# A bias table built with TensorE instead of VectorE, twelve modulation pieces moved to an earlier stage, and GpSimd's norm started later

## The chip, the cores and the metric

The kernel runs as one program on one core of a Trainium2 chip. The core has five engines, each with its own instruction stream: TensorE (PE, matmuls), VectorE (DVE), ScalarE (ACT), GpSimd (POOL) and SyncE (SP), which here only issues DMA transfers. The metric is the device time of one execution in microseconds, and less is better.

## The reference

A chain of six layers over one sequence of 256 tokens with 1024 features. The first block is four mixers with a residual and an RMS norm each: a conformer convolution, a forgetting attention, a short convolution, and a second conformer convolution. The second block has two layers, each of a token mixer (two attentions, gated and merged) and a convolutional feed-forward net, with a layer norm behind each and with a shift, scale and gate that come from a product with the large matrix `w_ada`:

```python
x = first_block(x, ...)                       # stages a0, b, c, a1
for l in range(DEPTH_2):                      # 2 layers: stages m0, f0, m1, f1
    mod = jax.nn.silu(c) @ w_ada[l] + b_ada[l]
    sh1, sc1, g1, sh2, sc2, g2 = jnp.split(mod[:, None, :], 6, axis=-1)
    h = x * (1.0 + sc1) + sh1
    y = token_mixer(h, positions, rel_bias, ...)
    x = layer_norm_2(DEEPNORM_ALPHA * x + g1 * y, ln1_g[l], ln1_b[l])
    h = x * (1.0 + sc2) + sh2
    y = conv_ffn(h, w_up[l], conv_w[l], conv_b[l], w_down[l])
    x = layer_norm_2(DEEPNORM_ALPHA * x + g2 * y, ln2_g[l], ln2_b[l])
```

What the change is about is the position bias of the first of the two attentions. For each of 8 heads, a query at position q and a key at position k get `rel_bias[t5_bucket(q - k)]`, where the bucket is the distance itself below 16, grows with its logarithm up to 128, and ends at 31:

```python
bias = rel_bias[t5_bucket(q_pos[:, :, None] - k_pos)]
logits = jnp.einsum('bqhd,bqkhd->bqkh', q, k_sel) * a_scale + bias
```

All arithmetic is in float32, and both layers of the second block use the same table.

## The kernel before

Activations stay on the chip; the weights, 332 MB, stream through it once. They are cut into 637 pieces, most of 128 rows by 1024 columns (0.52 MB). SP issues them in the order of a list that the functions `plan_a`, `plan_b`, `plan_c`, `plan_m` and `plan_f` write, into six buffers `raw`, so each transfer waits until the piece six places earlier has been used. A piece is one of three kinds. A **split** piece goes through ACT, which writes its high part `wh` (L107), and DVE, which writes the rest, `wl` = raw - wh (L114); TensorE then makes three matmuls of each 128x128 tile (high by high, high by low, low by high; L98), 24 matmuls of 256 columns for a piece. A **plain** piece is multiplied once, in slower float32. An **ada** piece belongs to `w_ada`: no matmul, but one DVE instruction over 128x1024 (L124 `raw<-raw,cb`) that multiplies by silu(c) and sums. Layer 0 of `w_ada` has 48 such pieces in stages b (28) and c (20); layer 1's 48 come in m0 (8, one behind each of its `qk` pieces) and f0 (40: two behind each `u` pair from i = 2 on). Which pieces lie where in the list is the whole schedule: ACT and DVE run through it up to three pieces ahead of the piece that TensorE is at (`feed_act`, `feed_dve`), and the wait for a semaphore before each use does the rest. Each engine's order is written out by hand, one function for each engine and stage (`pe_b`, `act_b`, `dve_b` and so on); an instruction behind a waiting one on its engine waits too.

The stages in order are a0, b, c, a1, m0, f0, m1, f1. Each begins with an **entry**: the norm, TensorE's transposes of X into PSUM (L101), then for each of 8 tiles a high part on ACT and a low part on DVE (`XS<-tmp,XS`, L114), and only then full matmuls. In m and f stages DVE's part of the entry is `dve_enter`. Stage b has values v0 to v2 (`values`), then keys and queries (`k`, `q`: eight pairs of pieces each), then v3, then 19 attention steps. Stage c runs over i = 0, 2, ..., 14; stages f over i = 0, 2, ..., 20, two halves each.

**The bias table.** `bias_step` (L1074) makes it in 305 DVE instructions: distances and buckets in 17, then for each of 32 buckets one mask of 128x384 and for each of 8 heads `table += mask * rel_bias` (128x384). They are fitted between other DVE work by calls `self.bias(dve, n)`: 6 behind each of v0 to v3, 5 behind each k and q pair, 2 + 2 in each attention step, 5 at each of four points of every i of stage c. In the trace they are the L124 groups `B<-B,C` and `B<-sc,C,B`, with some L119. The first reader is m0's attention (`dve_m`).

**GpSimd's norm.** Behind stages m0, f0 and m1, `pool_norm` (L1699) makes the next residual out of the normalised row: eight instructions X*g and X+b over 128x512. It waits for the next stage's transposes, which read X. The lines of the trace are `POOL L114 X<-X,B`.

**The head.** SP issues x in two halves, then one block of constants (2619 columns, 1.3 MB), the positions, six weight pieces and c. The first DVE work, the small `sm` instructions of the first norm, waits for the constants.

Of the kernel before, what the change touches and what calls it, by code (L numbers as in the profile page):

```python
# [347 lines left out]


class Net:  # L350

# [718 lines left out]
    def bias_views(self):  # L1070
        b = self.m["B"][2]
        return b[:, 0:3072].rearrange("p (h s) -> p h s", h=8), b[:, 3072:3456], b[:, 3456:3840]

    def bias_step(self, dve, n):  # L1074


        s, m = self.s, self.m
        Bz, dist, bk = self.bias_views()
        eq = [m["sc"][:], dist]
        up = s["bias"]  # L1080
        if n == 0:
            pf = self.tmp[5][:, 0:T + 2]
            dve.tensor_copy(pf, m["pos"][:]).then_inc(up.up("pf"), 1)
            dve.wait_ge(*up["pf"])
            for o, k, w in ((0, 0, 128), (128, 1, 256)):
                dve.ts(dist[:, o:o + w], pf[:, 0:w], pf[:, T + k:T + k + 1], -1.0, ALU.subtract,
                       ALU.mult).then_inc(up.up(("n", k)), 1)
            dve.wait_ge(*up["n", 1])
            dve.ts(dist, dist, 0.0, None, ALU.max, None).then_inc(up.up("n"), 1)
            dve.wait_ge(*up["n"])  # L1090
            dve.ts(bk, dist, 15.0, None, ALU.min, None).then_inc(up.up(("bk", 0)), 1)
        elif n <= 16:
            dve.wait_ge(*up["bk", n - 1])
            dve.stt(bk, dist, float(bucket_starts()[n - 1]), bk, ALU.is_ge, ALU.add).then_inc(up.up(("bk", n)), 1)
        else:
            b, h = (n - 17) // 9, (n - 17) % 9 - 1
            if h < 0:
                dve.wait_ge(*up["bk", 16])
                if b >= 2:
                    dve.wait_ge(*up["add", b - 2, 7])  # L1100
                dve.ts(eq[b % 2], bk, float(b), None, ALU.is_equal, None).then_inc(up.up(("mask", b)), 1)
            else:
# [1357 lines left out]
```

## Time and profile before

| | us |
|---|---|
| median of 3 runs | 2084.36 (2083.13 to 2084.97) |
| the profiled execution | 2082.0 |
| its span in the trace | 2080.2 |
| PE busy | 1895.7 (91%) |
| weight load (PEld) busy | 1702.1 (82%) |
| DVE busy | 1620.2 (78%) |
| ACT busy | 1079.7 (52%) |
| POOL busy | 301.1 (14%) |
| mean granted TensorE clock | 0.962 |
| bytes moved | 342 MB, 165 GB/s, the queue that carries them busy 50% |

The stages, by the moments at which one ends and the next begins: a0 0 to 254, b to 610, c to 858, a1 to 1102, m0 to 1360, f0 to 1603, m1 to 1862, f1 to 2080. TensorE is the busiest engine throughout. The numbers of one engine's busy time are sums over the whole span, and an engine that is idle behind another's result in one stage may be the bound in the next; so the profile is best read stage by stage, with the chain of waits to say who waited for whom. "Clock" is the TensorE clock that was granted, as a share of full speed (1.00 is 2.4 GHz, 0.50 is 1.2 GHz).

### The profile page before, as it was taken

Reading aid. Unit: us, or ns where it says so; the run is one execution under the profiler, and the core shown is the slowest. Engines: PE = TensorE matmul, PEld = TensorE weight load, DVE = VectorE, ACT = ScalarE, POOL = GpSimd, SP = SyncE. Lnnn points to the kernel's source line nnn. Section 1 sums busy time; section 2 is a strip of 40 time slices with the busy share of each in tenths; the row PEclk is TensorE's granted clock in tenths of the full one; section 3 lists DMA queues with packets and bytes.
Section 4 is the critical chain, followed back from the end, with each engine's and each line's share of the span. In section 5 each row is a group of like instructions: output and inputs, shape, how many; then the busy total and the mean of one; then the engine's idle time right before and its main releaser. Section 6 shows DMA issues by size and latency. Waiting matters only on the chain.

```text
span 2080.2 us, 32564 instructions
## 1 busy us (share of the span) xinstructions
PE 1895.7 (91%) x12370; PEld 1702.1 (82%) x12370; DVE 1620.2 (78%) x3041; ACT 1079.7 (52%) x1928; POOL 301.1 (14%) x380
## 2 busy tenths in 40 slices
PE   7897999989999999989979988988887987889997
PEld 6897888868889899889968876877886986779996
DVE  6988788978889998599976866778888576686666
ACT  6887644423354444478855444444445444454554
POOL 3876000000000000087800000020001000010000
PEclk9998999989999999999989999999999999999998
DMA  6344455634446776344535632537775352344652
GB/s 219 124 162 132 162 183 186 229 111 142 132 139 219 236 236 204 112 139 145 171 111 162 206 110 82 183 121 268 273 266 181 122 151 78 103 161 153 206 189 71
DMA packets 93756, 342.29 MB, mean 165 GB/s; under 512 B 10400, under 2 KB 10528, under 8 KB 92960
## 3 DMA queue, kind: packets, MB, share of 16 engines
q1 hardware_dynamic: 93600, 340.20, 49.9%
q8 instruction: 99, 1.62, 0.3%
q14 instruction: 57, 0.47, 0.1%
HBM read 339.11 MB, written 1.05 MB: 164 GB/s over the span
## 4 chain that ended last, share of the span: by engine, by line
PE 56%; DVE 30%; ACT 11%; issue 2%; DMA 0%; POOL 0%; SPq 0%; DVEq 0%; ACTq 0%
PE ps L98 55%; DVE wl L114 9%; ACT tmp L104 6%; DVE ps L124 5%; DVE tmp L124 3%; ACT wh L107 3%; DVE B L124 2%; DVE XS L114 2%; DVE tmp L114 1%; DVE B L114 1%; DVE tmp L119 1%; DVE raw L124 1%; ACT B L104 1%; DVE sm L136 1%; PE ps L101 1%
## 5 line engine op out<-in xcount | busy, mean ns | idle before, releaser
L98 PE MATMUL ps<-XS,wh 128*128 128x256 f32 (+1 forms) x5072 | 955.2, 290 | 39.9 <-DVE wl L114 27.4
L98 PEld LDWEIGHTS ps<-XS,wh 128*128 128x128 f32 (+1 forms) x5072 | 807.9, 195 | 65.4 <-issue 40.6
L114 DVE TENSOR_TENSOR wl<-raw,wh 128x1024 fp32r<-128x1024 f32 (+1 forms) x493 | 591.8, 1228 | 180.5 <-ACT wh L107 180.5
L98 PE MATMUL ps<-XS,wl 128*128 128x256 f32 (+1 forms) x2536 | 726.6, 287 | 0.0
L107 ACT CAST wh<-raw 128x1024 fp32r<-128x1024 f32 (+1 forms) x493 | 496.0, 1038 | 98.6 <-PE ps L98 92.8
L98 PEld LDWEIGHTS ps<-XS,wl 128*128 128x128 f32 (+1 forms) x2536 | 495.4, 195 | 0.0
L114 POOL TENSOR_TENSOR B<-B,tmp 128x236 f32<-128x236 f32 (+10 forms) x352 | 268.3, 800 | 775.1 <-ACT tmp L104 775.1
L98 PE MATMUL ps<-wh,os 128*128 128x512 f32 x864 | 291.0, 405 | 27.8 <-DVE os L114 18.9
L124 DVE SCALAR_TENSOR_TENSOR ps<-B,C,ps 128x254 f32<-128x254 f32 (+17 forms) x576 | 224.5, 469 | 8.3 <-ACT ps L104 8.3
L98 PEld LDWEIGHTS ps<-wh,os 128*128 128x128 f32 x864 | 167.9, 194 | 67.0 <-DVE os L114 20.8
L98 PE MATMUL ps<-wl,os 128*128 128x512 f32 x432 | 173.4, 401 | 0.0
L98 PE MATMUL ps<-B,raw 128*128 128x256 f32 x768 | 168.2, 379 | 0.0
L98 PEld LDWEIGHTS ps<-B,raw 128*128 128x128 f32 x768 | 145.1, 190 | 19.2
L114 POOL TENSOR_TENSOR X<-X,B 128x512 f32<-128x512 f32 x24 | 32.6, 1371 | 798.0 <-PE ps L101 797.0
L104 ACT ACTIVATE tmp<-B,C 128x236 f32<-128x236 f32 (+10 forms) x352 | 142.7, 477 | 8.7 <-POOL B L114 8.2
L124 DVE SCALAR_TENSOR_TENSOR tmp<-ps,C,tmp 128x254 f32<-128x254 f32 (+1 forms) x176 | 72.7, 475 | 89.4 <-ACT tmp L104 89.4
L104 ACT ACTIVATE B<-ps 128x512 f32<-128x512 f32 (+2 forms) x86 | 49.8, 584 | 154.9 <-PE ps L98 154.3
L104 ACT ACTIVATE tmp<-ps,C 128x256 f32<-128x256 f32 x88 | 45.0, 561 | 148.5 <-PE ps L98 148.5
L124 DVE SCALAR_TENSOR_TENSOR raw<-raw,cb 128x1024 f32<-128x1024 f32 x96 | 116.2, 1218 | 0.0
L104 ACT ACTIVATE tmp<-ps 128x384 f32<-128x384 f32 (+2 forms) x129 | 64.9, 510 | 95.6 <-PE ps L98 80.4
L98 PE MATMUL ps<-wh,XS 128*128 128x512 f32 x320 | 100.3, 391 | 0.5 <-DVE wl L114 0.4
L98 PEld LDWEIGHTS ps<-wl,os 128*128 128x128 f32 x432 | 84.4, 195 | 15.5
(155 smaller groups left out, 1950.2 us busy)
## 6 DMA issues: line engine op xcount, KB each, us to landing
raw<-in_w SPq DMA_DIRECT2D x623, 512.0 KB, 4.4
raw<-in_w SPq DMA_DIRECT2D x12, 384.0 KB, 3.9
B<-in_ln SPq DMA_DIRECT2D x4, 1024.0 KB, 6.8
C<-in_cst SPq DMA_DIRECT2D x1, 1309.5 KB, 8.2
X<-in_x SPq DMA_DIRECT2D x2, 512.0 KB, 4.6
out_x<-X SPq DMA_DIRECT2D x4, 256.0 KB, 2.5
cb<-in_cb SPq DMA_DIRECT2D x1, 512.0 KB, 13.2
raw<-in_w SPq DMA_DIRECT2D x2, 256.0 KB, 3.3
```

Source lines behind the costliest of these rows:

```text
L98: return NOTHING if self.e is None else self.e.matmul(*a, **k)
L101: return NOTHING if self.e is None else self.e.transpose(*a)
L104: return NOTHING if self.e is None else self.e.activation(*a, **k)
L107: return NOTHING if self.e is None else self.e.copy(*a)
L114: return NOTHING if self.e is None else self.e.tensor_tensor(o, a, b, op)
L119: return self.e.tensor_scalar(o, a, s1, s2, op0) if op1 is None else self.e.tensor_scalar(o, a, s1, s2, op0, op1)
L124: return self.e.scalar_tensor_tensor(out=o, in0=a, scalar=s, in1=b, op0=op0, op1=op1, **k)
L136: return NOTHING if self.e is None else self.e.tensor_reduce(o, a, AX, ALU.max)
```

## The change

Four parts.

1. **The table by TensorE.** Positions now come as 128x320: columns 0 to 255 hold the position of each query, the other 64 hold keys, four in a column group, each repeated over 32 partitions. A mask is one DVE instruction, 128 partitions (4 keys x 32 buckets) by 128 queries: is (query - key) at least the start of the partition's bucket? The constants `rblk` hold for each bucket the step of `rel_bias` from the bucket below, so one float32 matmul of a mask (stationary, 128x128) with `rblk` (moving, 32 columns) gives the bias of 4 keys by 8 heads for 128 queries. 96 masks and 96 matmuls make the table, through a ring of 6 mask buffers; every 16 matmuls fill one PSUM bank, and ACT copies it out (`act_bias`, six times). 32 masks stand on DVE ahead of stage a0's first norm (their matmuls are the first of TensorE's program, 16 in each of PSUM banks 6 and 7), and 64 stand in stage b, four behind each k and q pair (bank 3). All 305 former instructions are gone; the attention of m0 now waits for the sixth copy.
2. **The head's transfers.** The positions and 209 columns of constants (`NFIRST`) go first, then x, two weight pieces, the other 2219 columns, four weight pieces, c.
3. **Twelve ada pieces of layer 1** move from the end of f0 (i = 16, 18, 20 have none now) into stage c, where 32 of 32 places are filled instead of 20.
4. **GpSimd's norm** waits for `xlow[nxt, 7]`, the last of the next entry's low parts, instead of the transposes.

The places at which the instructions move are these. DVE at its very start, before the change: the small instructions of the first norm come first, then its application to X and the entry.

```order
L119 TENSOR_SCALAR sm<-sm 128x2
L124 SCALAR_TENSOR_TENSOR sm<-sm 128x2
L130 RECIPROCAL sm<-sm 128x2
L114 TENSOR_TENSOR sm<-sm 128x2
L124 SCALAR_TENSOR_TENSOR sm<-sm 128x2 x2
L119 TENSOR_SCALAR tmp<-X,sm 128x512 x2
L119 TENSOR_SCALAR B<-ps,C 128x256 x8
L114 TENSOR_TENSOR XS<-B,XS 128x256 x8
```

After the change, the same place (`B<-B,C` and `sc<-B,C` of 128x128 are masks; the rows left out repeat the pair):

```order
L131 CAST B<-pos 128x320
L118 TENSOR_TENSOR C<-C 128x32
L123 TENSOR_SCALAR B<-B,C 128x128 x3
L123 TENSOR_SCALAR sc<-B,C 128x128 x3
...
L123 TENSOR_SCALAR B<-B,C 128x128 x2
L123 TENSOR_SCALAR sm<-sm 128x2
L128 SCALAR_TENSOR_TENSOR sm<-sm 128x2
L134 RECIPROCAL sm<-sm 128x2
L118 TENSOR_TENSOR sm<-sm 128x2
L128 SCALAR_TENSOR_TENSOR sm<-sm 128x2 x2
```

32 masks and two conversions now stand ahead of the first norm. Next, TensorE in the k and q part of stage b, after the change; `ps<-tmp,C 16x256` are the row sums for the norm of k, which closed a pair before, too:

```order
L102 MATMUL ps<-XS,wh 128x256 x2
L102 MATMUL ps<-XS,wl 128x256
L102 MATMUL ps<-tmp,C 16x256 x2
L102 MATMUL ps<-C,B 128x32 x3
L102 MATMUL ps<-C,sc 128x32
L102 MATMUL ps<-XS,wh 128x256 x2
L102 MATMUL ps<-XS,wl 128x256
```

Four matmuls of 32 columns with a mask as stationary now follow them. DVE at the end of v3 in stage b, before (`B<-ps` is v3's own evacuation, `B<-B,C,ps 128x256` the scaling of k and q for a head, on which the first attention step waits):

```order
L124 SCALAR_TENSOR_TENSOR raw,mod<-raw,cb 128x1024
L127 COPY B<-ps 128x512
L119 TENSOR_SCALAR B<-B 128x384
L124 SCALAR_TENSOR_TENSOR B<-B,C 128x384 x5
L124 SCALAR_TENSOR_TENSOR B<-B,C,ps 128x256 x2
L124 SCALAR_TENSOR_TENSOR B<-B,C 128x384 x2
L124 SCALAR_TENSOR_TENSOR B<-B,C,ps 128x256 x2
```

and after:

```order
L128 SCALAR_TENSOR_TENSOR raw,mod<-raw,cb 128x1024
L131 COPY B<-ps 128x512
L128 SCALAR_TENSOR_TENSOR B<-B,C,ps 128x256 x4
L140 TENSOR_REDUCE sm<-ps 128x1 x2
```

The table's instructions between v3's evacuation and the scaling, and among the scalings, are gone. Last, DVE in stage c at the start of the table's rows of one iteration, before (`raw,mod<-raw,cb` is an ada piece):

```order
L124 SCALAR_TENSOR_TENSOR raw,mod<-raw,cb 128x1024
L114 TENSOR_TENSOR wl<-raw,wh 128x1024 x2
L114 TENSOR_TENSOR tmp<-ps,tmp 128x512
L124 SCALAR_TENSOR_TENSOR B<-sc,C,B 128x384 x5
L124 SCALAR_TENSOR_TENSOR raw,mod<-raw,cb 128x1024
L114 TENSOR_TENSOR wl<-raw,wh 128x1024 x2
L124 SCALAR_TENSOR_TENSOR tmp<-tmp,C 128x255 x2
L124 SCALAR_TENSOR_TENSOR tmp<-tmp,C 128x254 x2
L114 TENSOR_TENSOR tmp<-ps,tmp 128x512
L114 TENSOR_TENSOR wl<-raw,wh 128x1024 x2
```

and after, somewhat later in the same stage:

```order
L128 SCALAR_TENSOR_TENSOR raw,mod<-raw,cb 128x1024
L118 TENSOR_TENSOR wl<-raw,wh 128x1024 x2
L128 SCALAR_TENSOR_TENSOR raw,mod<-raw,cb 128x1024
L118 TENSOR_TENSOR wl<-raw,wh 128x1024 x2
L118 TENSOR_TENSOR tmp<-ps,tmp 128x512
L128 SCALAR_TENSOR_TENSOR raw,mod<-raw,cb 128x1024
L118 TENSOR_TENSOR wl<-raw,wh 128x1024 x2
L128 SCALAR_TENSOR_TENSOR tmp<-tmp,C 128x255 x2
L128 SCALAR_TENSOR_TENSOR tmp<-tmp,C 128x254 x2
L118 TENSOR_TENSOR tmp<-ps,tmp 128x512
L118 TENSOR_TENSOR wl<-raw,wh 128x1024 x2
```

Each run of five table instructions is gone, and every group of two `wl` has an ada piece ahead of it up to the last i.

The diff, without the lines of bookkeeping:

```diff
 CONSTS = (
-    [(f"a_norm{j}", 8) for j in range(2)]
+    [("bstart", 1), ("rblk", 32), ("rblk0", 32), ("a_norm0", 8), ("a_norm1", 8), ("ident", 128)]
...
+NFIRST = 209
...
-def plan_c(u):
+def plan_c(u, u1):
...
-            for _ in range(1):
-                a = next(u, None)
-                if a is not None:
-                    out.append(ada_piece(0, a))
+            a = next(u, None)
+            if a is not None:
+                out.append(ada_piece(0, a))
+            else:
+                out.append(ada_piece(1, next(u1)))
...
     def sp_program(self, e):
+        sp.dma_start(self.m["pos"][:], posr).then_inc(s["pos"].sem, 16)
+        sp.dma_start(self.m["C"][:, 0:NFIRST], cst[:, 0:NFIRST]).then_inc(s["const0"].sem, 16)
         for tb in range(2):
             sp.dma_start(self.X[:, tb, :], xin[:, tb, :]).then_inc(s[f"x{tb}"].sem, 16)
-        sp.dma_start(self.m["C"][:], cst).then_inc(s["const"].sem, 16)
-        sp.dma_start(self.m["pos"][:], posr).then_inc(s["pos"].sem, 16)
-        for i in range(NRAW):
+        for i in range(2):
+            self.load(sp, i)
+        sp.dma_start(self.m["C"][:, NFIRST:NCONST], cst[:, NFIRST:NCONST]).then_inc(s["const"].sem, 16)
+        for i in range(2, NRAW):
             self.load(sp, i)
...
     def pe_a(self, pe, j):
         if j == 0:
-            pe.wait_ge(*s["const"][0])
+            self.pe_bias(pe, 16, 6)
+            self.pe_bias(pe, 16, 7)
...
     def act_a(self, act, j):
         if j == 0:
             self.act_rms(act, A, lambda tb, h: s[f"x{tb}"][0], "a_norm0", True)
+            self.act_bias(act, 0, 6)
+            self.act_bias(act, 1, 7)
...
     def dve_a(self, dve, j):
         if j == 0:
-            dve.wait_ge(*s["const"][0])
+            self.dve_bias_begin(dve)
+            self.masks(dve, 32)
             dve.wait_ge(*s["x0"][0])
...
+    def masks(self, dve, n):
+        for _ in range(n):
+            x = self.nmask
+            self.nmask += 1
+            q, g = (0, x) if x < 32 else (128, x - 32)
+            if x >= RING:
+                dve.wait_ge(*s["table"][x - RING])
+            dve.ts(self.mask(x), pf[:, q:q + 128], pf[:, T + g:T + g + 1], self.c("bstart"), ALU.subtract,
+                   ALU.is_ge).then_inc(s["mask"].up(x), 1)
+
+    def pe_bias(self, pe, n, bank):
+        pe.wait_ge(*s["bias"]["steps"])
+        for _ in range(n):
+            x = self.nbias
+            self.nbias += 1
+            pe.wait_ge(*s["mask"][x])
+            if x > 32 and x % 16 == 0:
+                pe.wait_ge(*s["evac"]["bias", x // 16 - 1])
+            a = 32 * (x % 16)
+            pe.matmul(self.ps[bank][:, a:a + 32], self.mask(x), self.c("rblk", 0, 32), start=True, stop=True).then_inc(
+                s["table"].up(x), 1)
+
+    def act_bias(self, act, e, bank):
+        k0 = 64 * e if e < 2 else 128 + 64 * (e - 2)
+        act.wait_ge(*s["table"][16 * e + 15])
+        act.activation(Bz[:, :, k0:k0 + 64], self.ps[bank].rearrange("p (k h) -> p h k", h=8), ACT.Identity).then_inc(
+            s["evac"].up(("bias", e)), 1)
...
     def pe_b(self, pe):
                 if n:
                     squares(which, i - 2)
+                self.pe_bias(pe, 4, 3)
...
     def dve_b(self, dve):
                 for x in range(2):
                     self.feed_dve(dve, f"b.{which}{i}.{x}")
-                self.bias(dve, 5)
+                self.masks(dve, 4)
...
     def dve_c(self, dve):
-            self.bias(dve, 5)          # at four places of each i
...
     def pool_norm(self, pool, L):
         for h in range(2):
-            pool.wait_ge(*s["turn"][nxt, "in", 4 * h + 3])
+            pool.wait_ge(*s["xlow"][nxt, 7])
...
     def dve_m(self, dve, l):
-                    dve.wait_ge(*s["bias"]["add", 31, 7])
+                    dve.wait_ge(*s["evac"]["bias", 5])
```

## Rows read from the trace of the kernel before

**Rows 1.** Windows: a stretch's length, busy time of each engine (records), clock, DMA share, GB/s

```profile
312.00:364.00 52.00, 51.79 (x390) 45.49 (x390) 42.62 (x65) 23.69 (x33) 0.00 (x0) 1.00 0.56 186
...
617.14:857.47 240.33, 230.78 (x1721) 220.88 (x1720) 213.59 (x326) 102.84 (x130) 0.00 (x0) 0.99 0.65 213
...
780.00:832.00 52.00, 52.00 (x393) 50.04 (x392) 43.50 (x63) 22.84 (x30) 0.00 (x0) 1.00 0.63 204
...
1404.00:1560.00 156.00, 137.53 (x935) 123.49 (x934) 127.95 (x205) 70.59 (x102) 0.00 (x0) 1.00 0.78 269
...
1924.00:2028.00 104.00, 104.00 (x739) 98.10 (x738) 70.78 (x105) 55.74 (x82) 0.00 (x0) 1.00 0.60 198
```

**Rows 2.** Chain that ended last, head: start, us, what

```profile
1.64 8.21 DMA C<-in_cst
...
9.87 0.18 DVE sm L119
```

**Rows 3.** DVE groups by form: busy us, mean ns, idle before

```profile
L124 DVE SCALAR_TENSOR_TENSOR B<-B,C 128x384 f32<-128x384 f32 x128 | 71.8, 612 | 0.5
...
L119 DVE TENSOR_SCALAR tmp<-tmp,sm 128x128 f32<-128x128 f32 x48 | 13.7, 286 | 1.7
...
L119 DVE TENSOR_SCALAR X<-X,sm 128x512 f32<-128x512 f32 x8 | 4.0, 542 | 0.0
...
L119 DVE TENSOR_SCALAR tmp<-X,sm 128x512 f32<-128x512 f32 x8 | 3.5, 484 | 0.1
```

**Rows 4.** PE timeline: fp32 matmuls 128x128, and the instruction behind them

```profile
1378.26 1.95 PE L98 MATMUL ps<-C,mod 128*128 128x128 f32 x16
1379.96 0.48 PE L98 MATMUL ps<-XS,wh 128*128 128x256 f32 x2
```

**Rows 5.** Windows, columns as in rows 1: the first 10 us, and around values(3)

```profile
0.00:10.00 10.00, 0.00 (x0) 0.00 (x0) 0.13 (x1) 3.95 (x9) 0.20 (x4) 1.00 0.81 295
...
424.50:428.90 4.40, 0.85 (x5) 0.66 (x4) 4.38 (x9) 0.93 (x1) 0.00 (x0) 1.00 0.51 196
...
428.90:446.10 17.20, 17.15 (x54) 12.08 (x53) 9.82 (x27) 2.76 (x9) 0.00 (x0) 0.50 0.00 0
```

**Rows 6.** Chain, end of values(3) in stage b

```profile
424.52 3.53 DVE B L124 x7
```

**Rows 7.** Chain in stage c, two iterations

```profile
664.18 1.59 DVE tmp L124 x4
...
695.24 1.59 DVE tmp L124 x4
```

**Rows 8.** Chain in stage f0, two half-iterations

```profile
1426.14 5.99 PE ps L98 x48
...
1436.14 5.87 PE ps L98 x47
```

**Rows 9.** Chain, ends of f0 and f1: last matmuls, normalised row

```profile
1576.30 6.00 PE ps L98 x48
...
1602.41 0.92 DVE X L119 x2
...
2036.00 19.17 PE ps L98 x138
...
2071.06 0.52 DVE X L119 x2
```

**Rows 10.** Timelines: DVE entry of m0, then of f0, and POOL beside f0's

```profile
1106.01 0.99 DVE L119 TENSOR_SCALAR tmp<-ps,mod 128x256 f32<-128x256 f32 x2 [0.80 <-PE ps L101]
...
1111.62 0.43 DVE L114 TENSOR_TENSOR XS<-tmp,XS 128x256 fp32r<-128x256 f32 x1 [0.45 <-ACT XS L107]
...
1360.40 0.99 DVE L119 TENSOR_SCALAR tmp<-ps,fold 128x256 f32<-128x256 f32 x2 [0.53 <-PE ps L101]
...
1367.34 5.29 DVE L114 TENSOR_TENSOR XS<-tmp,XS 128x256 fp32r<-128x256 f32 x4
...
1361.17 11.18 POOL L114 TENSOR_TENSOR X<-X,B 128x512 f32<-128x512 f32 x8 [317.30 <-PE ps L101]
```

More of the change, by code:

```diff
@@ L151 @@
 SIGNALS = [
-    "const", "x0", "x1", "pos", "cb", "out",
+    "const", "const0", "x0", "x1", "pos", "cb", "out",
     "cast",
@@ L180 @@
     "bias",
+    "mask",
+    "table",
     "select",
@@ L341, in plan @@
     b, u = plan_b()
-    out = plan_a(0) + b + plan_c(u) + plan_a(1)
-    u = iter(range(48))
+    u1 = iter(range(48))
+    out = plan_a(0) + b + plan_c(u, u1) + plan_a(1)
+    u = u1
     for l in range(2):
@@ L741, in pair @@
             b = self.ps[bank[kind, p]]
+            if j == 0 and p == 1 and kind in "gv":
+                pe.wait_ge(*s["evac"]["bias", 0 if kind == "g" else 1])
             if (kind, p) in prior:
@@ L1071, in bias_views @@
         b = self.m["B"][2]
[L1072 to L1102, printed above, removed]
-                r = self.c("rel_bias", b * 8 + h)
-                dve.wait_ge(*up["mask", b])
-                if b == 0:
-                    dve.ts(Bz[:, h, :], eq[0], r, None, ALU.mult, None).then_inc(up.up(("add", b, h)), 1)
-                else:
-                    dve.wait_ge(*up["add", b - 1, h])
-                    dve.stt(Bz[:, h, :], eq[b % 2], r, Bz[:, h, :], ALU.mult, ALU.add).then_inc(
-                        up.up(("add", b, h)), 1)
@@ L1112, in bias, with mask, dve_bias_begin @@
-    def bias(self, dve, n):
-        for _ in range(n):
-            if self.nbias < 17 + 32 * 9:
-                self.bias_step(dve, self.nbias)
-                self.nbias += 1
+        return b[:, 0:3072].rearrange("p (h s) -> p h s", h=8), b[:, 3072:3072 + NPOS]
+    def mask(self, n):
+        i = n % RING
+        b = self.m["B"][2][:, 3392:3776] if i < 3 else self.m["sc"]
+        return b[:, (i % 3) * 128:(i % 3) * 128 + 128]
+    def dve_bias_begin(self, dve):
+        s = self.s
+        Bz, pf = self.bias_views()
+        dve.wait_ge(*s["pos"][0])
+        dve.tensor_copy(pf, self.m["pos"][:]).then_inc(s["bias"].up("pf"), 1)
+        dve.wait_ge(*s["const0"][0])
+        dve.tt(self.c("rblk", 0, 32), self.c("rblk", 0, 32), self.c("rblk0", 0, 32), ALU.subtract).then_inc(
+            s["bias"].up("steps"), 1)
+        dve.wait_ge(*s["bias"]["pf"])
@@ L1292, in act_b @@
             for n, i in enumerate(range(0, 16, 2)):
+                if n and n % 4 == 0 or (which == "q" and n == 0):
+                    self.act_bias(act, (3 if which == "q" else 2) + (1 if n and which == "q" else 0), 3)
                 for x in range(2):
@@ L2355, in build @@
         counted = net()
-        for n in ("x0", "x1", "const", "pos", "cb"):
+        for n in ("x0", "x1", "const", "const0", "pos", "cb"):
             counts[n].at[0] = 16
@@ L2402, in constants @@
         put(f"kv_norm{l}", vec(inp["kv_norm_g_2"][l]))
-    put("rel_bias", np.broadcast_to(np.asarray(inp["rel_bias_2"]).reshape(1, 256), (128, 256)))
+    rel = np.asarray(inp["rel_bias_2"], np.float32)
+    steps = np.zeros((2, 4, 32, 4, 8), np.float32)
+    for k in range(4):
+        steps[0, k, :, k, :] = rel
+        steps[1, k, 1:, k, :] = rel[:-1]
+    put("rblk", steps[0].reshape(128, 32))
+    put("rblk0", steps[1].reshape(128, 32))
+    put("bstart", np.tile(np.array([-4.0e9] + list(range(1, 16)) + bucket_starts(), np.float32), 4).reshape(128, 1))
     put("ident", np.eye(128, dtype=np.float32))
```

26 lines of the change are left out of this document (14 added, 12 removed).

## The prediction

> **What bounds the kernel now.** I read the busy share by stretches first, then the chain of waits in each stage, then the timelines at the stage borders. TensorE bounds most of it, but not everywhere. In the k/q part of stage b it is busy 51.79 of 52 us: what is added there is paid in full, and what DVE is spared there is worth nothing [rows 1]. Stage c is mixed: 52.00 of 52 us late in it, but 230.8 of 240.3 over the whole. Stage f0 is bound by a chain through DVE: 137.5 of 156 us, where the same stage of the next layer, f1, has 104.00 of 104. At the head nothing runs on TensorE until the constants are there [rows 2], and at each stage's start it waits for the entry [rows 10]. So the table (DVE time in b and c), the ada pieces (DVE time in f0) and GpSimd's norm touch three places where TensorE does wait, and the 64 new matmuls one where it doesn't.
>
> **Stage c, table gone.** The chain runs through DVE at one point of every i: the four `tmp<-tmp,C` start at 664.18 and 695.24, 31.06 us apart [rows 7]. The PE-bound rate is 393 matmuls in 52.00 us [rows 1], 0.1323 us each; the stage has 64 input pieces of 24 matmuls and 16 output pieces of 12 (512 columns), together 1728 (1721 recorded), so 228.6 us instead of 240.3: -11.7. Is DVE then fast enough? An i holds about 20 table instructions at a pitch near 0.53 us (five of 2.65 us), 10.6 us; without them DVE's 31.1 become about 20.5, under TensorE's 28.6. The later i, which had no ada pieces, now get four of 1.22 us (4.9 us) and are at the same 20.5. Their transfers: 14 pieces in 28.6 us are 257 GB/s, and f0 runs 269 now at a DMA share of 0.78 [rows 1]. I take -11.7 (bounds 0 and -13).
>
> **Stage b, table gone.** At the end of v3 DVE does 3.53 us of seven instructions before TensorE may start attention [rows 6]; two of them are the scaling of head 0 (2 x 0.475 us), the other five and a `B<-B` of 0.28 ahead are the table's. 0.28 + 5 x 0.53 is 2.9, of which 0.3 were hidden: -2.6. The next two scalings lose their two table instructions likewise: -1.0. A wait of 0.4 in v0 goes. Sum -4.0. That gap is also followed by 17.2 us at a granted clock of 0.50 (17.15 us busy; the 4.4 us before held 0.85 of PE work) [rows 5]. With less of a gap it may stay at 1.00, which would give up to half of 17.2, 8.6 us, but 2 us of the gap stay (v3's evacuation), so I count none of it and keep it for the range. The steady attention steps are TensorE's own, back to back; their table instructions cost nothing.
>
> **Stage b, 64 matmuls.** The trace has float32 matmuls of 128x128: eight (16 records) start at 1378.26, and the next instruction at 1379.96: 0.2125 us each, waits and weight load in it [rows 4]. 64 x 0.2125 = +13.6, in a stretch with no idle time to hide in. Bounds: 0.125 us each, what a 256-column matmul of a split piece takes (48 in 5.99 us [rows 8]), +8.0; and 0.2125 doubled at half clock, +27. TensorE shouldn't wait for masks: they are four of 0.26 us a pair on a DVE that is busy 42.6 of 52 and works ahead of it; the ring of six makes two of the four wait for the pair before, and they have a pair of pieces, 6 us, to be made in. Queued behind a waiting mask are DVE's low parts, which are up to three pieces ahead. ACT's four copies in b, some 0.6 us each, wait for matmuls that stand where ACT waited for TensorE anyway; it is busy 23.7 of 52. In the Trainium skill, "VectorE: DVE Perf Modes", section on the TRN2 errata, a matmul from SBUF takes the larger of 60 and 6 + columns cycles of 2.4 GHz, and the Trainium skill's "FP8 and Floating Point Precision" makes a true FP32 product four passes: for 32 columns that is an estimated 0.10 us, and the 64 would add 6.4. The trace agrees at 128 columns (4 x 134 cycles are 0.22, measured 0.2125) and has none of 32, so by the Trainium skill my term would be 7 us too high.
>
> **Head.** DVE's first norm instruction starts at 9.87, released by the constants' transfer (1.64 to 9.85) [rows 2]. Now two small transfers go first and masks start at an estimated 4.1 us. A mask's form isn't in the trace: 128x128 with one pointer is 0.286 us, and a second pointer adds 0.058 (0.542 against 0.484 at 128x512) [rows 3], 0.344 busy; neighbours overlap by about 0.08, pitch 0.26. 32 x 0.26 = 8.4, done at 12.5 against 9.87: +2.6. Bounds: pitch 0.20 gives +0.7, 0.344 gives +5.2. x (1 MB) is issued behind 0.27 MB of small transfers, less than the 1.3 MB that landed by 9.85, so it and ACT's squares lie under the masks. TensorE's clock was granted in full through 10 idle us at the start [rows 5]; but 32 sparse matmuls now lie before the dense part, and if that ends in a stretch at half clock like the one in b, another 5 to 8. I take +5, between both.
>
> **Stage f0, twelve pieces moved.** Two half-iterations begin at 1426.14 and 1436.14, 10.0 us apart, with 5.99 us of TensorE in each [rows 8]: the rest is ACT, DVE's combination and a low part in turn. f1, without ada pieces, is TensorE-bound: 739 matmuls in 104 us [rows 1], 8.5 per half against 10.0. Three i's lose all four: 6 halves x 1.5 = -9.0. The end of the stage is also slower than f1's: from the last half's matmuls (1576.30 + 6.00) to the normalised row at 1602.41, 20.1 us; in f1 from 2055.17 to 2071.06, 15.9: -4.2 [rows 9]. Sum -13.2 (bounds -7 and -15).
>
> **GpSimd behind the entry.** In m0 the entry on DVE runs from 1106.01 to 1112.05: 6.0 us, a low part takes 0.43. In f0 it runs from 1360.40 to 1372.63: 12.2 us, a low part takes 1.32, and beside it GpSimd's eight instructions of 1.37 us run back to back from 1361.17 [rows 10]. The scalings `tmp<-ps,fold` between them aren't stretched (0.53). f0, m1 and f1 have this: 3 x 6.2 = -18.6. Behind the entry DVE's next work is two low parts of weights that TensorE needs a unit later, then it waits for a first result: contention there costs +1 in all. The entry's shorter gaps should cut some of the half clock behind it, for which I choose -2 without a row to size it. Sum -19.6 (bounds -10 and -22). What GpSimd writes is the residual, read at the stage's end 200 us later, so its later start holds nobody. The Trainium skill, "SBUF — State Buffer", Terms, calls the port pair that DVE and GpSimd share an exclusive lock held for the full instruction, where the loser blocks. The trace agrees (0.43 becomes 1.32, about one GpSimd instruction more); by it the contention would follow GpSimd to every later DVE instruction with two SBUF inputs, which is rival A.
>
> **Sum.** -11.7 - 4.0 + 13.6 + 5 - 13.2 - 19.6 = -29.9 against the profiled 2082.0: 2052.1. The median of the runs lies 2.4 above the profiled one; with it 2054. A change under 0.2% (4.2 us) couldn't be told from none here.
>
> **Rivals.** A: the contention moves instead of going. Eight instructions of 1.37 us, 11 us a stage, now meet the first weights' low parts and the f stages' combination, on which f0's chain hangs [rows 8]. If every meeting is paid, the 19.6 are lost: 2074. For it: f0 has no slack on that chain. Against: the combination reads PSUM, like the scalings that weren't stretched; in m1 and f1 TensorE has slack behind the entry. 0.12.
> B: stage c stays as long as it is, because 257 GB/s with six buffers becomes its bound, or an ada piece holds a buffer longer: the 11.7 are not gained: 2066. For it: f0 at 269 GB/s does wait. Against: f0's waits end on DVE, not on a transfer. 0.08.
> C: slower. 64 sparse matmuls, four after each pair, bring TensorE's clock down in the k/q part, which now runs at 1.00 [rows 1]. That part is 32 pieces of 3.0 us and the 13.6 of the new ones, 110 us. Work at half clock takes twice as long; the gains of 29.9 and the 4.2 of resolution are used up when 34 us of this work, 68 us as they pass, are at half clock. With half of the part so it is 55 more: 2109. For it: in b the clock fell after a stretch with little PE work [rows 5]. Against: each group is under 1 us in 6.6 us of dense work. 0.04.
> D: the clock stays up where I counted it down: after v3 (up to -8.6) and at the head (-2.4): 2043. For it: the gap shrinks from 4.4 us to under 2. Against: the same clock falls at stage ends with gaps as short. 0.12.
>
> **Numbers.** Forecast 0.64, A 0.12, B 0.08, C 0.04, D 0.12. The likeliest gives 2054. Its own terms move it by 8 either way; with D below and B above, 2041 to 2068 leaves out A's far part, C, and a little below. A, B and D are all faster, so faster is 0.95; within 0.2% 0.01, slower 0.04.
>
> **What would show it.** Head: norm start near 12.5. k/q part: 64 short matmuls of 0.21 us, clock 1.00, no waits for `mask`. The start of attention about 3 us sooner after v3, and whether half clock follows. Stage c near 229 us with its chain on PE. f0: halves of 8.5 us for i from 16 on, 16 us from its last matmul to the norm. DVE's entry of 6 us in f0, m1, f1, with GpSimd behind it. I am wrong if matmul groups wait on masks, if stage c stays above 236 us, or if low parts behind the entries stretch and TensorE waits for them.

## The result, and the profile after

| | before | after |
|---|---|---|
| median, us | 2083.74 (2082.37 to 2084.97, 4 runs) | 2053.07 (2048.21 to 2053.18, 4 runs) |
| ratio after / before | | 0.9847, 95% interval 0.983 to 0.9864 |
| the profiled execution, its span | 2082.0, 2080.2 | 2048.2, 2046.4 |
| PE busy | 1895.7 (91%) | 1900.3 (93%) |
| DVE busy | 1620.2 (78%) | 1490.9 (73%) |
| mean granted clock | 0.962 | 0.973 |

The forecast was 2054, in a range of 2041 to 2068. DVE lost 129 us of busy time, TensorE gained 5 by the records, and the kernel became 31 us shorter. The execution that was profiled is the fastest of the four after, 5 us under the others, so I compare it stage by stage, and with two later traces of the same kernel (e1, e9), whose medians are 2055.43 and 2048.05: what one kernel's runs give differs by some 7 us from set to set.

The first transposes of each stage's entry (L101 before, L105 after) are its clock marks. Their rows in the timeline of PE before, for c, a1, f0, m1 and f1 (start, us, line, operation, count; in brackets the idle time ahead and who ended it):

```profile
613.96 1.06 PE L101 MATMUL ps<-C,tmp 128*128 128x128 f32 x8 [0.55 <-ACT tmp L104]
...
863.18 2.60 PE L101 MATMUL ps<-C,tmp 128*128 128x128 f32 x16 [0.55 <-ACT tmp L104]
...
1359.95 1.55 PE L101 MATMUL ps<-C,X 128*128 128x128 f32 x10 [1.43 <-DVE X L119]
...
1603.40 1.55 PE L101 MATMUL ps<-C,X 128*128 128x128 f32 x10 [0.23 <-DVE X L119]
...
1862.05 1.55 PE L101 MATMUL ps<-C,X 128*128 128x128 f32 x10 [1.44 <-DVE X L119]
```

and after, for a0, b, c, a1, f0, m1 and f1:

```profile
17.79 3.65 PE L105 MATMUL ps<-C,tmp 128*128 128x128 f32 x16
...
265.13 1.07 PE L105 MATMUL ps<-C,tmp 128*128 128x128 f32 x8 [1.17 <-ACT tmp L108]
...
627.50 1.06 PE L105 MATMUL ps<-C,tmp 128*128 128x128 f32 x8 [0.55 <-ACT tmp L108]
...
862.52 2.60 PE L105 MATMUL ps<-C,tmp 128*128 128x128 f32 x16 [0.56 <-ACT tmp L108]
...
1363.33 1.55 PE L105 MATMUL ps<-C,X 128*128 128x128 f32 x10 [1.42 <-DVE X L123]
...
1587.32 1.55 PE L105 MATMUL ps<-C,X 128*128 128x128 f32 x10 [0.25 <-DVE X L123]
...
1838.19 1.55 PE L105 MATMUL ps<-C,X 128*128 128x128 f32 x10 [1.78 <-DVE X L123]
```

a0's stood at 12.16 before, b's at 258.84, m0's at 1105.59 and 1107.76. The time from one mark to the next:

| kernel, traced once each | head | a0 | b | c | a1 | m0 | f0 | m1 | f1 and end |
|---|---|---|---|---|---|---|---|---|---|
| before | 12.2 | 246.7 | 355.1 | 249.2 | 242.4 | 254.4 | 243.4 | 258.6 | 218.1 |
| after | 17.8 | 247.3 | 362.4 | 235.0 | 245.2 | 255.6 | 224.0 | 250.9 | 208.2 |
| after again (e1) | 17.8 | 250.8 | 365.1 | 235.0 | 245.9 | 257.1 | 224.2 | 253.8 | 208.5 |
| after again (e9) | 17.8 | 246.4 | 364.0 | 235.0 | 244.2 | 255.9 | 223.9 | 251.0 | 208.2 |

c, f0 and f1 repeat within 0.3 us. a0, b, a1, m0 and m1 move by 1.5 to 4.4 us from trace to trace of one kernel. a1, which neither the change nor an experiment touches, runs from 241.4 to 245.9 us over all of them.

Windows of the kernel after; columns as in [rows 1]: the two in the head, the k/q part, the half-clock stretch behind v3, and stage c's matmuls. They answer to [rows 1, 5]:

```profile
0.00:10.00 10.00, 6.07 (x29) 6.10 (x29) 6.20 (x21) 3.92 (x9) 0.21 (x4) 1.00 0.79 269
...
4.00:17.79 13.79, 13.77 (x65) 13.66 (x65) 11.56 (x39) 3.71 (x11) 0.00 (x0) 1.00 1.01 399
...
310.00:362.00 52.00, 52.00 (x406) 47.23 (x405) 26.38 (x49) 21.38 (x29) 0.00 (x0) 1.00 0.52 178
...
449.20:459.80 10.60, 10.55 (x35) 7.66 (x35) 4.10 (x16) 2.62 (x9) 0.00 (x0) 0.52 0.00 0
...
630.48:858.68 228.20, 228.20 (x1730) 220.39 (x1730) 165.34 (x224) 104.51 (x133) 0.00 (x0) 1.00 0.75 252
```

c is now all TensorE, 228.20 of 228.20 us; the k/q part was full before and is full now; behind v3 the stretch at half clock is 10.2 us long (0.52 on average over the 10.6 shown) instead of 17.1.

The head, timeline of DVE, then of PE. These answer to [rows 2]:

```profile
3.44 0.85 DVE L123 TENSOR_SCALAR B<-B,C 128x128 f32<-128x128 f32 x3
...
5.85 1.20 DVE L123 TENSOR_SCALAR sc<-B,C 128x128 f32<-128x128 f32 x3
...
7.13 1.20 DVE L123 TENSOR_SCALAR B<-B,C 128x128 f32<-128x128 f32 x3
...
15.50 0.16 DVE L123 TENSOR_SCALAR sm<-sm 128x2 f32<-128x2 f32 x1
```

```profile
3.93 1.46 PE L102 MATMUL ps<-C,B 128*128 128x32 f32 x6 [3.93 <-DVE B L123]
...
14.16 1.47 PE L102 MATMUL ps<-C,B 128*128 128x32 f32 x6
```

The first nine masks come at DVE's own 0.26 us; from 5.85 on three take 1.28 (5.85 to 7.13), because the ring is full and TensorE makes a matmul only every 0.427 us. So the norm starts at 15.50 instead of 9.87.

A group of table matmuls in the k/q part, timeline of PE, answering to [rows 4]:

```profile
335.85 0.41 PE L102 MATMUL ps<-C,B 128*128 128x32 f32 x2
336.10 0.83 PE L102 MATMUL ps<-C,sc 128*128 128x32 f32 x6
336.76 0.48 PE L102 MATMUL ps<-XS,wh 128*128 128x256 f32 x2
```

A float32 matmul leaves two records; these are 8 records, four matmuls, from 335.85 to 336.76: 0.228 us each. The same instruction takes 0.427 in the head.

f0's entry, timelines of DVE and (last row) POOL, answering to [rows 10]:

```profile
1363.78 0.99 DVE L123 TENSOR_SCALAR tmp<-ps,fold 128x256 f32<-128x256 f32 x2 [0.53 <-PE ps L105]
...
1367.71 1.18 DVE L118 TENSOR_TENSOR XS<-tmp,XS 128x256 fp32r<-128x256 f32 x3
...
1369.33 0.43 DVE L118 TENSOR_TENSOR XS<-tmp,XS 128x256 fp32r<-128x256 f32 x1 [0.45 <-ACT XS L111]
...
1370.28 4.23 DVE L118 TENSOR_TENSOR wl<-raw,wh 128x1024 fp32r<-128x1024 f32 x2 [0.52 <-ACT wh L111]
...
1374.43 1.64 DVE L128 SCALAR_TENSOR_TENSOR tmp<-ps,C,tmp 128x255 f32<-128x255 f32 x4
...
1377.18 2.19 DVE L118 TENSOR_TENSOR wl<-raw,wh 128x1024 fp32r<-128x1024 f32 x1 [1.11 <-ACT wh L111]
...
1369.90 12.86 POOL L118 TENSOR_TENSOR X<-X,B 128x512 f32<-128x512 f32 x7 [323.92 <-DVE XS L118]
```

The entry now lasts from 1363.78 to 1369.76, 6.0 us, as in m0. What stood in it stands behind it: GpSimd's eight instructions take longer than before, and the low parts of weights beside them 2.1 us each instead of 1.2. The combination `tmp<-ps,C,tmp`, which reads PSUM, isn't stretched (four in 1.64). The entries of m1 and f1 last 6.0 us, too (1587.76 to 1593.73 and 1838.64 to 1844.63).

The end of f0, two rows of the chain of waits and one of DVE's timeline, answering to [rows 8, 9]:

```profile
1511.25 6.00 PE ps L102 x48
...
1521.26 48.51 PE ps L102 x348
...
1586.24 1.00 DVE L123 TENSOR_SCALAR X<-X,sm 128x512 f32<-128x512 f32 x2
```

The half at 1511.25 is the last that takes 10.0 us. From 1521.26 TensorE runs 48.51 us without a wait: five halves and the 48 matmuls of the sixth, which took 5 x 10.0 + 6.0 = 56.0 before. From their end at 1569.77 to the normalised row at 1586.24 are 16.5 us, where [rows 9] had 20.1.

### The profile page after: what moved, and what is told of

Same layout as the page of the kernel before. It is cut to its first block, busy times and chain, and to the rows that moved or that the text cites. A ratio compares the mean times of both kernels' runs of the same rounds, so it can differ in the third digit from the quotient of the medians.

```text
span 2046.4 us, 32747 instructions
## 1 busy us (share of the span) xinstructions
PE 1900.3 (93%) x12562; PEld 1717.9 (84%) x12562; DVE 1490.9 (73%) x2830; ACT 1082.5 (53%) x1934; POOL 306.4 (15%) x380
## 3 DMA queue, kind: packets, MB, share of 16 engines
q8 instruction: 100, 1.64, 0.3%
## 4 chain that ended last, share of the span: by engine, by line
PE 28%; DVE 14%; ACT 7%; issue 1%; DVEq 0%; ACTq 0%
PE ps L102 28%; DVE wl L118 5%; ACT tmp L108 4%; ACT wh L111 2%; DVE tmp L128 2%; DVE tmp L118 1%; DVE ps L128 1%; DVE sm L140 1%; DVE tmp L123 1%; DVE B L118 1%; ACT XS L111 1%; ACT B L108 1%; DVE X L128 0%; DVE sc L149 0%; DVE sm L123 0%
## 5 line engine op out<-in xcount | busy, mean ns | idle before, releaser
L102 PE MATMUL ps<-XS,wh 128*128 128x256 f32 (+1 forms) x5072 | 945.1, 288 | 17.9 <-DVE wl L118 14.8
L118 DVE TENSOR_TENSOR wl<-raw,wh 128x1024 fp32r<-128x1024 f32 (+1 forms) x493 | 604.3, 1253 | 244.1 <-ACT wh L111 244.1
L118 POOL TENSOR_TENSOR X<-X,B 128x512 f32<-128x512 f32 x24 | 39.8, 1675 | 773.2 <-DVE XS L118 772.2
```

Source lines behind the costliest of these rows:

```text
L102: return NOTHING if self.e is None else self.e.matmul(*a, **k)
L118: return NOTHING if self.e is None else self.e.tensor_tensor(o, a, b, op)
```

## The experiments

Each kernel ran four or five times beside the kernel before on the same chip; the ratio is to that. It goes by all the runs, so it can differ from that of the medians by some us. The stages are from one trace each.

**e1, the kernel after, again.**

> The changed kernel itself once more, so that the others stand beside it on one chip, and so that there is a second trace of it. Its four runs so far gave 2048.2 once and 2053.0 to 2053.2 three times; the trace belongs to the 2048.2. Expected: 2053 and, where the trace of the faster run had the granted clock at half for 11 us behind v3 in stage b, a longer such stretch here (17 us as before the change would be 3 more). Stages c, f0, m1, f1 as in the first trace within 1 us.

2055.43 (2052.37 to 2061.27), ratio 0.9877 (0.9857 to 0.9898). Stages in the table above. c, f0 and f1 repeat. m1, which I expected within 1 us, is 2.9 longer, and the stretch behind v3 is 13.7 us long.

**e2, TensorE woken ahead of the masks.**

```diff
+            for _ in range(8):
+                pe.matmul(self.ps[7][:, 0:128], self.m["rep"][0][:, 0:128], self.m["rep"][0][:, 128:256], ...)
             self.pe_bias(pe, 16, 6)
```

> Eight float32 matmuls of 128x128 on a zeroed tile (memset by DVE at the start) stand ahead of the first table matmul; nothing else differs. Theory H: TensorE still runs at half speed in the first 20 us although the profile's clock row says 1.00 there (a table matmul takes 0.427 us in the head and 0.228 in the k/q part, a transpose 0.43 against 0.25 in a later entry), so it, not DVE, sets the pace of the 32 masks. With it awake the masks run at DVE's 0.26, end near 12 instead of 15.5, and the kernel gains 3 to 5 us: about 2049. Rival: the pace of 0.427 is the round trip of mask, matmul and ring of six, or a contention with the transfers of the head; then the matmuls take the same time and the start is 0 to 1 us later: 2053 to 2054.

2055.47, ratio 0.9863 (0.9841 to 0.9885). Timeline of PE in its head:

```profile
1.18 3.79 PE L103 MATMUL ps<-rep 128*128 128x128 f32 x16 [1.18 <-DVE rep L138]
...
5.66 0.83 PE L103 MATMUL ps<-C,sc 128*128 128x32 f32 x6
...
7.00 0.83 PE L103 MATMUL ps<-C,sc 128*128 128x32 f32 x6
...
9.20 1.47 PE L103 MATMUL ps<-C,B 128*128 128x32 f32 x6
```

and windows there:

```profile
4.00:8.00 4.00, 4.00 (x32) 4.00 (x32) 3.79 (x16) 1.09 (x3) 0.00 (x0) 1.00 0.93 349
...
8.00:12.00 4.00, 4.00 (x25) 4.00 (x24) 3.68 (x15) 1.58 (x6) 0.00 (x0) 0.60 1.02 420
```

Once woken, six table matmuls take 1.34 us (5.66 to 7.00), 0.223 each, and DVE makes a mask every 0.257. Then, at about 9, the clock falls, and a matmul takes 0.427 again. So theory H holds: 0.427 is the time of such a matmul at half clock, not a round trip and not the transfers, which were about as dense around 6 us (0.93 over 4 to 8 us). It also shows two things that I had not expected: the clock column of the kernel after reads 1.00 over 4 to 17.8 us while its matmuls run at exactly this slow pace; and the clock fell while table matmuls alone ran, with PE busy 4.00 of 4.00 us by the records. The transposes came at 15.38 instead of 17.78, 2.4 us gained of the 3 to 5; the medians, 2055.47 and e1's 2055.43, don't show it.

**e3, the 64 matmuls of the k/q part twice.**

```diff
+            if x >= 32:
+                pe.matmul(self.ps[bank][:, a:a + 32], self.mask(x), self.c("rblk", 0, 32), start=True, stop=True)
             pe.matmul(self.ps[bank][:, a:a + 32], self.mask(x), self.c("rblk", 0, 32), start=True, stop=True).then_inc(
```

> Each of the 64 table matmuls of the k/q part is made twice (the second writes the same values). My theory: such a matmul costs its full time there, 0.213 us by the prediction and 0.228 by the trace after, so +14 us: 2067. Rival, by the smallest time of a matmul in the Trainium skill (0.10 us for four passes of 32 columns): +6.4, 2059.5. Rival, that the group's cost is the wait for its masks and not the matmuls: 0 to +3.

2064.2, ratio 0.9922 (0.9899 to 0.9945); beside e1 +8.8 by the medians, which lies between the theory's 14 and the rival's 6.4 and can't tell them apart. The stage can: its b lasts 376.3 us, where the kernel after has 362.4, 365.1 and 364.0. The period of a pair is clearer still. Two neighbouring row sums in the kernel before, timeline of PE:

```profile
313.11 1.04 PE L98 MATMUL ps<-tmp,C 128*16 128x256 f32 x4
...
320.01 1.04 PE L98 MATMUL ps<-tmp,C 128*16 128x256 f32 x4
```

and in e3:

```profile
327.54 1.04 PE L102 MATMUL ps<-tmp,C 128*16 128x256 f32 x4
...
336.24 1.04 PE L102 MATMUL ps<-tmp,C 128*16 128x256 f32 x4
```

A pair takes 6.90 us before, 8.70 here, and 7.81 in the kernel after (319.27 to 327.08): 0.9 for every four matmuls, 0.22 to 0.23 each, in both steps. My theory holds, and the rival's 0.10 each isn't there. The clock stayed up in the k/q part.

**e4, GpSimd released by the transposes.**

```diff
-            pool.wait_ge(*s["xlow"][nxt, 7])
+            pool.wait_ge(*s["turn"][nxt, "in", 4 * h + 3])
```

> The changed kernel with GpSimd's norm released by the transposes again, as before. My theory: three entries get 6.2 us longer each and half clock comes back behind them, less 1 us of contention saved elsewhere: +19.6, so 2073; from the trace of the changed kernel (m1 and f1 gained 7.8 and 9.9 with nothing else changed in them) rather +24, 2077. Rival A (contention only moves): the same time as the changed kernel, 2053.

2072.3, ratio 0.9952 (0.9933 to 0.997); +16.9 beside e1. By stage: f0 231.6 (+7.6), m1 259.5 (+6 to +9), f1 215.3 (+7.1), 20 to 23 in all; ahead of f0 only a1 differs, 241.5 us, with the same code. Windows of its three entries, from about the transposes on:

```profile
1359.60:1390.00 30.40, 26.61 (x166) 23.98 (x167) 20.96 (x27) 14.04 (x26) 10.86 (x8) 0.78 0.21 70
...
1591.00:1625.00 34.00, 28.59 (x203) 25.82 (x204) 22.27 (x25) 16.39 (x26) 10.87 (x8) 0.90 0.28 89
...
1850.00:1885.00 35.00, 31.38 (x198) 28.12 (x199) 26.35 (x36) 20.93 (x35) 10.85 (x8) 0.80 0.24 77
```

and of the kernel after, the same lengths from its transposes:

```profile
1363.30:1393.70 30.40, 27.35 (x209) 25.77 (x210) 26.25 (x40) 18.91 (x32) 13.92 (x8) 1.00 0.40 117
...
1587.30:1621.30 34.00, 32.69 (x265) 31.04 (x266) 20.09 (x27) 19.62 (x31) 11.99 (x8) 1.00 0.43 136
...
1838.20:1873.20 35.00, 33.73 (x254) 31.84 (x255) 27.93 (x41) 23.05 (x38) 13.92 (x8) 1.00 0.44 136
```

With GpSimd in the entry the clock falls in each: 0.78 of 30.4 us is 13 us at half speed. With GpSimd behind it the clock doesn't fall at all in the trace of the kernel after; in e1's and e6's it falls for 3.4 us in f0 and in f1. Rival A is refuted: the time comes back with the wait. GpSimd's own busy time shows that it, too, is held up now: 10.9 in e4, 12 to 14 after.

**e5, the twelve ada pieces back in f0.**

```diff
-            else:
-                out.append(ada_piece(1, next(u1)))
```

> The changed kernel with the twelve ada pieces of layer 1 back at the end of f0. My theory: f0's last three iterations return to 20 us each and its end to 20 us; by the prediction +13.2, by the stage table of the runs so far (f0 was 243.4 before and 224.0 after, of which the norm of GpSimd accounts for 7.6) +11.8: f0 about 236, the kernel 2065 to 2067. Stage c stays at 235.0. Rival B (stage c is held up by its transfers, four more per iteration): c becomes 2 to 6 us shorter and the loss is only 6 to 10.

2062.83, ratio 0.9894 (0.9868 to 0.992). f0 235.0 (+11.1), c 235.03 against 235.02. The twelve ada pieces in the later iterations of c cost nothing there, with the table gone: rival B is refuted, and their whole gain is f0's. What they would cost beside the table in c was not run. f1 was 3 us longer in this trace; its code is the same, and the clock fell for 6.8 us in its entry.

**e6, the kernel before with GpSimd's later start alone.**

> The kernel before with the later start of GpSimd's norm alone. If the parts add up, it gains what e4 showed in the changed kernel: f0 -7.6, m1 -6 to -8.6, f1 -7.1 (23 us in all), so about 0.989 of before. If the gain in f0 hangs on the ada pieces being gone (contention meets the chain through DVE, rival A in its weaker form), f0 gains under 4.

2066.24, ratio 0.9893 (0.9863 to 0.9922). f0 234.7 (-8.7), m1 253.3 (-5.4), f1 208.5 (-9.6): 23.7 us, as much as in the changed kernel. So the parts add up in f0: 243.4 - 8.7 - 11.1 = 223.6, measured 224.0. One changed wait in the program gives more than half of what the whole change gives: 17.5 us by the medians, 22 by the ratio.

e5 and e6, side by side on one chip, also price the table, which no run has alone: e5 is GpSimd's wait with the table and the head's transfers, e6 the wait without them. Their ratios are 0.9894 and 0.9893, their medians 3.4 us apart, within the noise. The stages say the same: +5.6 at the head, +7.7 in b with the 64 matmuls in it, -14.2 in c, -0.9 in all. Making the table by TensorE gains nothing that can be measured by itself; what is gained comes from GpSimd's wait and from the ada pieces.

**e7 and e10, 16 masks at the head and 80 in the k/q part** (with e2's eight matmuls).

```diff
-            self.masks(dve, 32)
+            self.masks(dve, 16)
...
-                self.pe_bias(pe, 4, 3)
+                self.pe_bias(pe, self.share(which, n), 3)     # 6, 5, 5, 6, 5, 5, ..., 0
```

> 16 instead of 32 masks ahead of the first norm, TensorE awake by the eight matmuls on a zeroed tile, and the other 80 in the first 15 of the 16 k/q pairs (6, 5, 5), each group of 16 copied out a pair later. My theory: the clock fell in the second run only after some 15 sparse matmuls, so all 16 run at DVE's pace and end near 8; the first transposes start near 10.5 instead of 17.8 (-7), stage b gets 16 x 0.22 = 3.5 longer: -3.5 net, about 2050. Rival: x and its squares are the next bound, transposes at 12 or later, and the net is 0 to -2.

> The kernel of e7 beside the changed one. The head is 5.6 us shorter there (transposes at 12.2 instead of 17.8); b was 5 to 8 longer instead of the 3.5 that 16 matmuls cost, of which I put 2 to 4 on the clock's chance. If so, 2 us faster than the changed kernel on one chip; if b is always 5 or more longer, the same time.

e7: 2051.58, ratio 0.983 (0.9805 to 0.9855). e10: 2047.79, ratio 0.9829 (0.981 to 0.9849), beside e9, the kernel after on the same chip:

> The changed kernel itself beside the next three on one chip. Expected as before: 2053 to 2055, stage c 235.0, f0 224.0, f1 208.4; a0, b, a1 and m0 differ by up to 4 us from run to run with where the granted clock falls to half.

2048.05, 0.9837 (0.9813 to 0.9861). The head of e10, timeline of PE:

```profile
5.90 1.47 PE L103 MATMUL ps<-C,sc 128*128 128x32 f32 x6
...
11.69 3.65 PE L106 MATMUL ps<-C,tmp 128*128 128x128 f32 x16
```

The transposes come 6 us sooner than after (5.6 in e7, at 12.18, where I expected 10.5), but b lasts 370.4 and 370.6 us, 5 to 8 more than after instead of 3.5. The rest is the clock behind v3: the stretch at half clock there is 17.1 us long in both traces, against 10.2 in the kernel after's. The net is nothing that can be measured. The matmuls that should wake TensorE failed here in both runs (0.427 a matmul at 5.90), though the same eight worked in e2; why isn't settled.

**e11, the same without them.**

> The kernel of e10 without the eight matmuls on a zeroed tile. In e7 those did not wake TensorE in time (table matmuls took 0.427 us behind them) and only delayed it: the first table matmul stood at 4.76 instead of 3.9. Without them the transposes should start at about 11.3 instead of 12.2: 0.5 to 1 us faster than e10, and no more. If e7's cold start was a chance and the clock is mostly up by 4.8, this one is up to 2 us slower.

2048.96, ratio 0.9837 (0.9816 to 0.9858). Transposes at 12.68, later than e10's 11.69; the last wait ahead of them is for ACT, not for TensorE's table matmuls (ended by 11.0). The squares of x's second half start at 9.15 here, held by its transfer, and at 8.15 in e10. So at the head x and its squares are the next bound in this trace, as e7's rival said, and my half to one microsecond wasn't there. The b of 366.1 is 3.7 more than after's 362.4, what 16 matmuls cost, and its stretch behind v3 is 10.2 us long as there.

**e12, no masks at the head** (a third of the table is left at zero).

> The changed kernel without the 32 masks and matmuls at the head and their two copies (a third of the table is left at zero, written by one DVE memset behind the entry). It prices them: if x and its squares were ready before, the transposes start at 11 to 12 and not at 17.8, so 6 to 7 us are their whole price; the prediction counted 5 against the kernel before, whose transposes stood at 12.2. If they start under 10.5, the new order of transfers is a gain of its own that the masks hide.

2047.28, ratio 0.9831 (0.9804 to 0.9858), 0.8 us under e9 by the medians; the span of its trace is 2039.6, e9's 2046.3. First norm instruction, timeline of DVE, and the transposes, timeline of PE:

```profile
9.36 0.17 DVE L123 TENSOR_SCALAR sm<-sm 128x2 f32<-128x2 f32 x1 [5.80 <-ACT tmp L108]
...
12.01 3.65 PE L105 MATMUL ps<-C,tmp 128*128 128x128 f32 x16 [12.01 <-ACT tmp L108]
```

The transposes stand at 12.01, so the 32 masks cost 5.8 us by the traces (the medians don't show it), and the new order of transfers gains nothing by itself: before, they stood at 12.16, held by the constants; now x, behind the small transfers, holds them.

**e8, GpSimd released still later.**

```diff
-            pool.wait_ge(*s["xlow"][nxt, 7])
+            pool.wait_ge(*s["gemm"][late])      # m1: the third qk piece; f0, f1: u4.0.1
```

> The changed kernel with GpSimd's norm released still later, by the third attention weight piece of m1 and by the piece f.u4.0.1 in f0 and f1. Theory: the contention follows GpSimd to every DVE instruction with two operands in SBUF (a low part of weights took 2.1 us instead of 1.2 beside it); in f0, whose halves hang on a low part each, it then costs a little more (0 to +4), in m1 and f1 nothing (low parts have slack). So 0 to +4 in all, with the entries still at 6 us. Rival: behind the entry is as bad a place as any, and a later one gains 1 to 3 us in m1 and f1.

2064.15, ratio 0.9895 (0.987 to 0.992), 4 to 12 us slower than the kernel after by the ratios. f0 226.4 (+2.4), as expected; f1 208.4; but m1 258.3, +5 to +7, where I expected nothing. Timelines of DVE and POOL there:

```profile
1640.31 3.67 DVE L118 TENSOR_TENSOR wl<-raw,wh 128x1024 fp32r<-128x1024 f32 x2 [5.43 <-ACT wh L111]
...
1639.39 11.76 POOL L118 TENSOR_TENSOR X<-X,B 128x512 f32<-128x512 f32 x6 [216.87 <-PE ps L102]
```

The low parts stretch to 1.8 us beside DVE's attention work, TensorE's wait for an `sm` of DVE becomes 3.43 us instead of 1.58, and 6.8 us at half clock follow. Beside GpSimd TensorE is busy 9.82 of 11.76 us here, and 10.19 of 14.0 in f0. Behind the entry, in the kernel after, it is busy 13.90 of 13.90 us in f0, 11.91 of 12.00 in m1 and 13.82 of 13.90 in f1, though DVE isn't idle there (11.88, 6.33 and 11.88 us busy). So that place is good because TensorE isn't made to wait, and it isn't a matter of later being better.

## Why the prediction came out right, point by point

| step | predicted | measured |
|---|---|---|
| head | +5 | +5.6 (three traces) |
| b, matmuls | +13.6 | +14.6 (64 x 0.228); e3: +0.9 for each four, +14.4 |
| b, table gone | -4.0 | about -7: the eight traces with 64 matmuls there average 364.0, the two of before and e6 356.3; +7.7, less 14.6 |
| c | -11.7 | -14.2 |
| f0, twelve pieces | -13.2 | -11.1 (e5), -11.8 (e4 against before) |
| GpSimd behind the entry | -19.6 | -23.7 (e6), -20 to -23 (e4) |
| a0, a1, m0 | 0 | +5 together in the first trace, +10 in e1, +3 in e9, +1 in e12 |
| all | -29.9 | -30.7 by the medians |

That the sum is right within 1 us is luck: its terms, as measured, miss by -3.0, -2.5 and -4.1 on one side and by +0.6, +1.0, +2.1 and +5 on the other. What the runs bear out is each mechanism and its size within 2 to 5 us, and the range.

**Head: the right size for a wrong reason.** I took a mask rate of 0.26 us on DVE (+2.6) and another 5 to 8 for a stretch at half clock in the dense part behind it, and chose +5 between. The mask was priced right (0.343 us busy, one every 0.257), and no such stretch was added: in the first trace a0 is 0.6 us longer than before. What happened is that TensorE was at half speed from its first instruction, so the masks waited for its 0.427 us: 32 x 0.427 is 13.7 us from 3.9 on. [rows 5] reads 1.00 over the first 10 us, and I took that for a clock granted in full. It isn't evidence: the trace of e2 shows a matmul at full speed for comparison. The transposes have the sign in them, too, in the rows above: 16 records in 3.65 us at 17.79, 8 in 1.07 at 265.13; the kernel before has the same pair of durations at 12.16 and 258.84.

**c: a misread end.** The stage's matmuls run from 616.90 to 859.34 before, 242.4 us, and I took 240.3. After, they take 228.2; the forecast of TensorE's part was 228.6. So 2.1 of the 2.5 us are my reading of the end, 0.4 the rate.

**b: the clock behind v3 came back sooner.** I left up to 8.6 us there out of the sum and put it into the range. The stretch is 17.1 and 20.5 us long before and in e6, and 10.2 to 13.7 in the eight traces, 12.8 on average: 6.0 less, worth 3 by an estimate, since TensorE is busy all through it (10.55 of 10.60 us above) and a matmul at half clock takes twice as long. That is the 3 us by which the table's going gave more than 4.0.

**f0 and GpSimd: two errors that partly cancel.** The halves gave 56.0 - 48.5 = 7.5 and not 9.0, since the sixth half's last part, its combination, was counted in the end of the stage as well: the end then gave 20.1 - 16.5 = 3.6, not 4.2. Together 11.1, as e5 has it. The entries gave their 18.6 as forecast, and 5.1 of e6's 23.7 are left for the clock and the rest, where I chose -2 without a row and +1 for contention. The clock is at half for 10.2 us in each of the three entries before and for 34 us in all in e4's; after, for none, and in e1 and e6 for 6.8 in all. No run separates it from the rest.

**The rivals.** A falls by e4 and e6. Its mechanism is real (low parts go from 1.2 to 2.1 us beside GpSimd, PSUM readers stay), but the DVE instructions that it meets behind the entry have slack; e8 shows the same mechanism at a place where they have not. The Trainium skill, "SBUF — State Buffer", "Who interferes with whom", has the rule that DVE instructions with two SBUF inputs contend with GpSimd's reads; this case's traces agree, by the same numbers. A low part of the entry lost 0.9 us (0.43 to 1.32), though, less than the one GpSimd instruction of 1.37 that the prediction reads into it. B falls by e5. C didn't occur in the k/q part (1.00 over 310 to 362, and no fall in all of it), but in e2's head the clock did fall while table matmuls alone ran. D is what happened in part, behind v3; at the head it didn't.

## What to carry to other kernels

Ask of an off-path engine not how late its work may be, but whose work can bear to be stretched when it runs: one wait moved by some 5 us gave 17 to 23 us, and replacing 305 DVE instructions by 96 masks and matmuls, by itself, none that can be measured. A stage bound through DVE (f0) can give DVE work to one bound by TensorE (c) and gain the whole of its price. And time the same instruction at two places before you believe a clock column or a single row.

## What the runs showed of the hardware that I had not expected

- A float32 matmul of 32 columns with a new 128x128 stationary takes 0.223 to 0.228 us, no less than one of 128 columns (0.2125 in [rows 4]), and 0.427 at the lower of TensorE's two clock levels. The Trainium skill's minimum ("VectorE: DVE Perf Modes", the section on the TRN2 errata) would give an estimated 0.10 in four passes; the measurement decides.
- Until the first change is recorded in a trace, the granted clock reads 1.00, also where TensorE runs at half speed; the column is no evidence there. In the kernel after, the records of float32 matmuls of 256 columns start 0.427 us apart up to 22.5 us and 0.216 apart from there, where the first change stands (four records and seven in 1.2 us below); the column reads 1.00 on both sides:

```profile
21.30:22.50 1.20, 1.20 (x4) 0.94 (x4) 1.20 (x4) 1.16 (x4) 0.00 (x0) 1.00 0.00 0
...
22.80:24.00 1.20, 1.20 (x7) 1.07 (x6) 1.20 (x5) 1.18 (x3) 0.00 (x0) 1.00 0.00 0
```

- In e2 the clock fell while such matmuls filled all of TensorE's time by the records (4.00 of 4.00 us), and in the kernel after 13.8 us of them went by at half speed; between dense pieces, 0.9 us in 7.8, they did no harm (1.00 over the k/q part).
